# First mixer: the fill jobs around the heads multiplied in split form and in parts, four weight slots, and the second layer's modulation moved into the feed-forward stage

## The reference, cut to what matters

```python
# first block: one layer
proj = x @ w_in                       # da_q da_k da_v r_q r_k r_v r_g m_q and three gates
y_da  = diff_attention(da_q, da_k, da_v)          # 8 heads, two softmaxes a head
y_ret = silu(r_g) * retention(r_q, r_k, r_v)      # 4 heads
m_k, m_v = split(mem @ w_mem_kv)
y_mem = memory_attention(m_q, m_k, m_v)           # 4 heads
merged = sum_n(sigmoid(gate_n + b_gate_n) * (branch_n @ w_branch[n]))
x = layer_norm(alpha * x + merged @ w_o)
x = layer_norm(alpha * x + hier_moe(x))           # 16 experts, 2 per token
# second block: two layers; c is one row of 1024
for l in range(2):
    sh_m, sc_m, g_m, sh_f, sc_f, g_f = split(silu(c) @ ada_w[l] + ada_b[l])
    y = mixer_l(x * (1 + sc_m) + sh_m)            # even_mixer, then spatial gating
    x = layer_norm(alpha2 * x + (1 + g_m) * y)
    h = x * (1 + sc_f) + sh_f
    y = swiglu(h) if l == 0 else moe_swiglu(h)    # width 2816; then 8 experts of 3584
    x = layer_norm(alpha2 * x + (1 + g_f) * y)
```

## Time and profile before

| | us |
|---|---|
| median of 3 runs (2226.83 to 2230.08) | 2227.34 |
| the profiled execution | 2237.93 |
| its span, first to last instruction | 2236.1 |
| busy in the span: PE | 2138.5 (96%) |
| DVE | 1721.6 (77%) |
| ACT | 1383.4 (62%) |
| POOL | 29.9 (1%) |
| first mixer, to the first expert's chunks | about 535 |
| dense feed-forward stage | 932 to 1128 |

### The profile page before, as it was taken

The page is one execution under the profiler, slowest core; times in us unless marked ns, Lnnn a source line. Parts: engine busy times, 40 slices in busy tenths (PEclk is TensorE's granted clock), DMA queues, the critical chain, the costliest instruction groups (busy, mean ns, idle before and its releaser), DMA issues.

```text
span 2236.1 us, 26692 instructions
## 1 busy us (share of the span) xinstructions
PE 2138.5 (96%) x10668; PEld 1802.2 (81%) x10668; DVE 1721.6 (77%) x2065; ACT 1383.4 (62%) x1672; POOL 29.9 (1%) x30
## 2 busy tenths in 40 slices
PE   8999999989999988899988999999999999999997
PEld 7758889888888876778868888888888888888886
DVE  2566577777999876544456799999999999999988
ACT  3345344625778755443443678877877788878774
POOL 0000000000000000000000000000000000000000
PEclk9999999997999999899999799999999999999999
DMA  9656559547999973145440799999999999999994
GB/s 354 260 222 247 209 223 357 208 185 285 383 390 381 384 274 113 61 150 204 192 185 16 283 388 373 387 367 389 360 392 369 380 384 365 380 371 391 371 394 165
DMA packets 58071, 659.17 MB, mean 295 GB/s; under 512 B 6096, under 2 KB 12112, under 8 KB 18896
## 3 DMA queue, kind: packets, MB, share of 16 engines
q1 hardware_dynamic: 50832, 633.49, 72.8%
q0 software_dynamic: 3696, 13.63, 1.5%
q10 hardware_dynamic: 3408, 10.22, 1.2%
HBM read 645.79 MB, written 11.53 MB: 294 GB/s over the span
## 4 chain that ended last, share of the span: by engine, by line
PE 83%; DVE 9%; DMA 4%; ACT 3%; issue 2%; DVEq 0%; ACTq 0%; SPq 0%
PE psum L2193 55%; PE psum L1982 8%; PE psum L1940 7%; PE psum L1920 3%; DVE stage_lo L1700 2%; DMA ring<-moe_w_down_in 2%; PE psum L1972 2%; PE psum L2328 1%; PE psum L1899 1%; DVE ring L1363 1%; DMA ring<-moe_w_up_in 1%; DVE mixer_split L1467 1%; PE psum L2092 1%; PE psum L2203 1%; PE psum L2005 0%
## 5 line engine op out<-in xcount | busy, mean ns | idle before, releaser
L1700 DVE TENSOR_TENSOR stage_lo<-ring,stage_hi 128x1024 fp32r<-128x1024 f32 (+1 forms) x934 | 1099.4, 1217 | 107.7 <-ACT stage_hi L1245 94.0
L1245 ACT ACTIVATE stage_hi<-ring 128x1024 fp32r<-128x1024 f32 (+1 forms) x934 | 955.4, 1054 | 276.3 <-PE psum L2193 159.6
L2193 PE MATMUL psum<-stage_hi,x_hi 128*128 128x512 f32 (+1 forms) x1344 | 530.8, 395 | 3.6 <-DVE arena L1830 2.6
L2193 PE MATMUL psum<-stage_hi,x_lo 128*128 128x512 f32 (+1 forms) x1344 | 522.5, 389 | 0.0
L2193 PE MATMUL psum<-stage_lo,x_hi 128*128 128x512 f32 (+1 forms) x1344 | 521.0, 388 | 0.0
L2193 PEld LDWEIGHTS psum<-stage_hi,x_hi 128*128 128x128 f32 x1344 | 253.3, 188 | 53.8 <-issue 4.7
L2193 PEld LDWEIGHTS psum<-stage_hi,x_lo 128*128 128x128 f32 x1344 | 253.1, 188 | 53.5
L2193 PEld LDWEIGHTS psum<-stage_lo,x_hi 128*128 128x128 f32 x1344 | 253.6, 189 | 49.2
L2193 PE MATMUL psum<-stage_hi,h_hi 128*128 128x512 f32 x664 | 261.1, 393 | 2.7 <-DVE h_lo L1842 2.7
L2193 PE MATMUL psum<-stage_lo,h_hi 128*128 128x512 f32 x664 | 258.7, 390 | 0.0
L1940 PE MATMUL psum<-mixer_split 128*128 128x256 f32 x1184 | 194.3, 293 | 18.4 <-DVE mixer_split L1467 9.2
(11 more groups left out here) (264 smaller groups left out, 2091.1 us busy)
## 6 DMA issues: line engine op xcount, KB each, us to landing
ring<-moe_w_gate_in SPq DMA_DIRECT2D x56, 2048.0 KB, 9.8
ring<-moe_w_up_in SPq DMA_DIRECT2D x56, 2048.0 KB, 10.0
ring<-moe_w_down_in SPq DMA_DIRECT2D x56, 2048.0 KB, 9.9
ring<-w_in SPq DMA_DIRECT2D x48, 2048.0 KB, 9.9
ring<-ada_w_in SPq DMA_DIRECT2D x16, 2048.0 KB, 8.8
ring<-w_in_in SPq DMA_DIRECT2D x10, 2048.0 KB, 11.7
mixer_tiles<-w_in_in SPq DMA_DIRECT2D x9, 2048.0 KB, 9.6
mixer_tiles<-ada_w_in SPq DMA_DIRECT2D x8, 2048.0 KB, 8.8
```

Of the source, the lines that this page charges most:

```text
L1245: act.activation(chunk_view(stage_hi, f, side, p, c), chunk_source(f, side, p, c), ACT.Copy)\
L1700: dve.tensor_tensor(chunk_view(stage_lo, f, side, p, c), chunk_source(f, side, p, c), chunk_view(stage_hi, f, side, p, c).bitcast(F32), AL ...
L2193: ins = pe.matmul(dst, a, b, start=start, stop=stop)
```

## The change

Five things are done together.

1. All fill jobs of the attention heads, and m_q, become split jobs. `HEAD_FILL` gives each head its jobs, `HEAD_CHUNKS` their four chunks. New steps `("part", job, c)` let PE multiply one chunk at a time; the job's own gemm step does what is left. ACT's high parts are steps `("hi", job, c)` placed by hand among the parts of the head before, DVE's low parts of the first two chunks follow the norm, and those of the last two are made inside `da_score`, behind the maximum, while ACT takes the exponentials.
2. `da_turn` stands ahead of the head's last part instead of directly ahead of `da_out`.
3. The first mixer has four slots; the fifth one's place holds the four homes of high parts. The high part of x goes to mem's tile, so ACT loads mem later, at the first `("split", "x_late", 0)`. The stage of gate1 has no wait for the last `ret_out` any more.
4. Only the first layer's 12 ada panels stay in the first mixer: one between da_v's two pairs, one in each retention head, the rest from gate1 to the third memory head.
5. The second layer's modulation is made in the dense feed-forward stage. POOL loads 24 halves of panels, 1 MB each, into two buffers in the arena, each half when DVE has summed the one two before; DVE does one sum of 1024 behind each of 48 low parts (`sum_half`), and then bias and 1.

```diff
+HEAD_FILL = ((("r_q", 0), ("r_q", 1)), (("r_k", 0), ("r_k", 1)), (("r_v", 0),), (("r_v", 2),), (("r_g", 0), ("r_g", 1)),
+             (("r_g", 2), ("r_g", 3)), (("gate0", 0), ("gate0", 1)), (("gate0", 2), ("gate0", 3)))
+
+def chunks_in(job):
+
+    return 4 if job[0] in TURNED else 2
+
+HEAD_CHUNKS = [[(job, c) for job in jobs for c in range(chunks_in(job))] for jobs in HEAD_FILL]
...
+    def part(job, c):
+
+        if c < chunks_in(job) - 1:
+            return [("part", job, c)]
+        return gemms(job[0], *((job[1], job[1] + 1) if job[0] in TURNED else (job[1],)))
+
...
-    s += gemms("da_v", 0, 1, 2, 3) + [("lam", 0, 0)] + ada(0, 1)
-    fill = [q for name, n in (("r_q", 2), ("r_k", 2), ("r_v", 4), ("r_g", 4), ("gate0", 4)) for q in gemms(name, *range(n))]
+    s += gemms("da_v", 0, 1) + ada(0) + [(side, *HEAD_CHUNKS[0][c]) for side in ("hi", "lo") for c in range(2)]
+    s += gemms("da_v", 2, 3) + [("lam", 0, 0)] + [("hi", *HEAD_CHUNKS[0][c]) for c in (2, 3)]
     for h in range(DA_H):
-        s += [("da_score", h, 0), ("da_score", h, 1), fill.pop(0)]
+        now = HEAD_CHUNKS[h]
+        nxt = HEAD_CHUNKS[h + 1] if h + 1 < DA_H else []
+        s += [("da_score", h, 0), ("da_score", h, 1)] + [("hi", *q) for q in nxt[:1]] + part(*now[0])
+        s += part(*now[1]) + [("hi", *q) for q in nxt[1:2]]
         if h:
             s += [("da_norm", h - 1, 0)]
-        s += [fill.pop(0), ("da_turn", h, 0)] + ada(2 + h) + [("da_out", h, 0)]
+        s += [("lo", *q) for q in nxt[:2]] + part(*now[2]) + [("hi", *q) for q in nxt[2:3]]
+        s += [("da_turn", h, 0)] + part(*now[3]) + [("hi", *q) for q in nxt[3:4]] + [("da_out", h, 0)]
...
-        s += [fill.pop(0)] + ada(10 + h) + [("ret_mean", h, 0)]
+        s += [fill.pop(0)] + ada(1 + h) + [("ret_mean", h, 0)]
...
-        s += [("mem_out", h - 1, 0)] + ada(18 + h)
+        s += [("mem_out", h - 1, 0)] + (ada(9 + h) if h < 3 else [])
...
-        s += gemms("branch2", i) + splits("merged", i) + (ada(22 + i) if i < 2 else [])
+        s += gemms("branch2", i) + splits("merged", i)
...
-HI_HOMES = ([M_HI + n * 1024 for n in range(4)], [M_FREE + n * 1024 for n in range(4)],
+HI_HOMES = ([SLOT + n * 1024 for n in range(4)], [16384 + n * 1024 for n in range(4)],
...
-        plan_loads(n, SLOTS)
+        plan_loads(n, SLOTS if n else SLOTS - 1)
...
+        def half_loads():
+
+            pool.wait_ge(job_done, done[("ln_back", 2, 3)])
+            for j in range(24):
+                if j > 1:
+                    pool.wait_ge(ada_half_summed, j - 1)
+                nc.gpsimd.dma_start(ada_half[j % 2].rearrange("p a b -> p (a b)"),
+                                    w["ada_w_2"][1, j // 2][:, j % 2 * 2 * D:(j % 2 + 1) * 2 * D]).then_inc(ada_half_in[j % 2], 16)
...
+                        if i == 0:
+                            act.wait_ge(*last_use["x"])
+                            act.dma_start(memT.rearrange("p k t -> p (k t)"), w["mem"][0]).then_inc(mem_in, 16)
...
+        def sum_half(m):
+
+            j, c = m // 2, 48 + m
+            if m % 2 == 0:
+                dve.wait_ge(ada_half_in[j % 2], 16 * (j // 2 + 1))
+            wt = ada_half[j % 2][:, m % 2, :]
+            ins = dve.tensor_tensor_reduce(wt, wt, cond_row, 1.0, 0.0, ALU.mult, ALU.add, mod[:, c:c + 1])
+            if m % 2:
+                ins.then_inc(ada_half_summed, 1)
+            if m == 47:
+                dve.wait_ge(ada_half_summed, 24)
+                shift_modulation(1)
...
                     dve.tensor_reduce(dmax, logit, AX.X, ALU.max, negate=True).then_inc(da_logits, 1)
+                    job, c = HEAD_CHUNKS[a][2 + i]
+                    staged_low(("lo", *job), *staged_chunks(("lo", *job))[c])
                     dve.wait_ge(da_exped, u + 1)
...
+                    if not f["routed"] and 0 <= n - STAGES < 48:
+                        sum_half(n - STAGES)
```

More of the change, by code:

```diff
@@ L110, in shape_constants @@
     return out
-SPLIT = ("da_k", "da_v", "gate1", "m_k", "m_v", "branch1", "gate2", "branch2", "w_o")
-TURNED = ("da_v", "m_v", "ev_p", "od_v")
-SPLIT_OF = {"da_k": "x", "da_v": "x", "gate1": "x_late", "gate2": "x_late", "m_k": "mem", "m_v": "mem",
+SPLIT = ("da_k", "da_v", "m_q", "gate1", "m_k", "m_v", "branch1", "gate2", "branch2", "w_o")
+TURNED = ("da_v", "r_v", "m_v", "ev_p", "od_v")
+HEAD_FILL = ((("r_q", 0), ("r_q", 1)), (("r_k", 0), ("r_k", 1)), (("r_v", 0),), (("r_v", 2),), (("r_g", 0), ("r_g", 1)),
[3 more added lines that the diff above has]
+HEAD_CHUNKS = [[(job, c) for job in jobs for c in range(chunks_in(job))] for jobs in HEAD_FILL]
+SPLIT_OF = {"da_k": "x", "da_v": "x", "r_q": "x", "r_k": "x", "r_v": "x", "r_g": "x", "gate0": "x", "m_q": "x", "gate1": "x_late", "gate2": "x_late", "m_k": "mem", "m_v": "mem",
             "branch1": "yret", "branch2": "ymem", "w_o": "merged", "ev_q": "h1", "ev_p": "h1", "ev_o": "mix1",
@@ L125, in with_stages @@
     jobs = [n for n, q in enumerate(steps) if q[0] == "gemm" and not (q[1] in TURNED and q[2] % 2)]
+    made = [q[1] if q[0] == "hi" else q[1:] for q in steps if q[0] in ("hi", "stage")]
     at = {}
     for before, n in zip(jobs, jobs[1:]):
-        if steps[n][1] not in SPLIT:
+        if steps[n][1] not in SPLIT or steps[n][1:] in made:
             continue
@@ L170, in mixer1_steps @@
         s += [("ret_out", h, 0)] + (splits("x_late", 0, 1, 2, 3) if h == RET_H - 1 else [])
-        s += [fill.pop(0)] + ada(10 + h) + [("ret_mean", h, 0)]
+        s += [fill.pop(0)] + ada(1 + h) + [("ret_mean", h, 0)]
         s += ([("ret_score", h + 1, 0)] if h + 1 < RET_H else []) + [fill.pop(0), ("ret_var", h, 0)]
-    s += gemms("gate1", 0, 1) + splits("mem", 0, 1, 2, 3) + gemms("gate1", 2, 3) + ada(14)
-    s += gemms("m_k", 0, 1) + ada(15) + gemms("m_k", 2, 3) + ada(16)
-    s += gemms("m_v", 0, 1) + ada(17) + gemms("m_v", 2, 3) + splits("yret", 0, 1, 2, 3) + ada(18)
+    s += gemms("gate1", 0, 1) + splits("mem", 0, 1, 2, 3) + gemms("gate1", 2, 3) + ada(5)
+    s += gemms("m_k", 0, 1) + ada(6) + gemms("m_k", 2, 3) + ada(7)
+    s += gemms("m_v", 0, 1) + ada(8) + gemms("m_v", 2, 3) + splits("yret", 0, 1, 2, 3) + ada(9)
     s += [("mem_score", 0, 0)] + gemms("branch1", 0)
@@ L402, in build @@
     cond_row = scratch(M_ADA, D)
+    ada_half = [region(at, 2, D) for at in (R_K, R_V)]
     router = (small[:, 160:320].rearrange("p (k e) -> p k e", e=G1 + N1),
@@ L471, in build @@
     ada_summed = sem("ada_summed")
+    ada_half_in, ada_half_summed = [sem(f"ada_half_in{n}") for n in range(2)], sem("ada_half_summed")
     w_hi_set, w_lo_set, w_used = sem("w_hi_set"), sem("w_lo_set"), sem("w_used")
@@ L547, in build @@
         for s in plan:
-            if s[0] in ("ada", "stage", "hi", "lo", "split", "lam", "sg_norm"):
+            if s[0] in ("ada", "stage", "hi", "lo", "part", "split", "lam", "sg_norm"):
                 continue
@@ L913, in _ @@
             for k, one in enumerate(loads[n]):
-                if n == 0 and k == SLOTS:
+                if n == 0 and k == SLOTS - 1:
                     small_loads()
@@ L1005, in walk @@
                     for n, c in staged_chunks(q) if kind == "stage" else staged_chunks(q)[i:i + 1]:
-                        if s == ("stage", "gate1", 0):
-                            act.wait_ge(job_done, done[("ret_out", RET_H - 1, 0)])
                         if hi_free[n]:
@@ L1011, in walk @@
                     continue
-                if kind in ("lo", "sg_norm"):
+                if kind in ("lo", "part", "sg_norm"):
                     continue
@@ L1327, in _ @@
             act.wait_ge(job_done, plan_end[n])
[L1328 removed]
+            act.wait_ge(ada_summed, 12)
             if feeds[n]["routed"]:
@@ L1901, in turn4, with split_product @@
             ins.then_inc(job_done, 1)
-        def split_product(s):
+        opened = {}
+        def split_product(s, parts):
             _, a, i = s
@@ L1909, in split_product @@
                 nxt = ("gemm", a, i + 1)
-                banks = [open_bank(s), open_bank(nxt)]
-                for n, c in staged_chunks(s):
+                if 0 in parts:
+                    opened[s] = [open_bank(s), open_bank(nxt)]
+                banks = opened[s]
+                for n, c in [staged_chunks(s)[m] for m in parts]:
                     pe.wait_ge(w_lo_set, n + 1)
@@ L1926, in split_product @@
                 return
-            if s == ("gemm", "ev_o", 0):
+            if s == ("gemm", "ev_o", 0) and 0 in parts:
                 for m in range(2):
@@ L1931, in split_product @@
                     evacuated(("gqa_out", n, 0))
-            b = open_bank(s)
-            for m, (n, c) in enumerate(staged_chunks(s)):
+            if 0 in parts:
+                opened[s] = open_bank(s)
+            b = opened[s]
+            for m, (n, c) in [(m, staged_chunks(s)[m]) for m in parts]:
                 pe.wait_ge(w_lo_set, n + 1)
@@ L1945, in _ @@
         pe.wait_ge(ones_set, 2)
+        begun = {}
         def walk(plan):
@@ L1948, in walk @@
```

(7 more changed lines are left out.)

21 lines of the change are left out of this document (12 added, 9 removed).

## The result

The changed kernel takes 2211.64 us (median of 4 runs, 2208.3 to 2213.78), the kernel before 2228.71 in the runs beside it: ratio 0.9919, 95% interval 0.9905 to 0.9932, a gain of 17 to 18 us. A second comparison (`after_again`) gave 0.9907 (0.9892 to 0.9922), some 21 us. Faster, then, but by about half of the 37 us forecast. The profiled execution has a span of 2211.9 us against 2236.1.

What follows compares the result with a forecast made beforehand. PE, nearly always busy, was taken to bound the kernel by its work and few holes. Terms -9.1 - 9.9 - 8.0 - 4.7 - 12.5 + 1 + 6 = -37.2 gave 2200.7 profiled, 2190 timed; forecast 2182 to 2198, range 2176 to 2213.

Steps and rivals of the forecast that it cites:

- heads: Attention heads: split fill jobs and moved ada panels save 9.1 us in head 0, 9.9 in 1-3, 8.0 in 4-7.
- retention heads: Retention: four m_q jobs become split jobs and DVE's work still fits under PE's, -4.7 us.
- tail behind the memory heads: End of the memory branch: without three ada panels, PE's holes and the clock drop go, -12.5 us.
- four slots: First mixer's panel queue: m_k's second panel and gate2's are asked for late, +1 us, bounds 0 and 4.
- feed-forward stage: Dense feed-forward: sums are free, but DVE waits for contended half loads, +6 us, bounds 0 and +36.
- The bound of 4: First mixer: the most, in us, that going to one slot fewer was expected to cost.
- By hand through one pair: Feed-forward pair walked: two waits of about 3 us, 3.5 free, about 2.4 left, in 2.6 pairs: +6.
- the upper bound: Feed-forward with all half loads contended: 12 x 14.2 = 170 against PE's 134 us, +36.
- Half loads or ACT bind harder: Rival: feed-forward waits of 20 us and more, or ACT stretching the heads; gain 8 to 28, 2199 to 2219; chance 0.26.
- All hidden: Rival: PE also sets heads 4 to 7 at 14.6 each, loads are free; -51, 2176 us; chance 0.17.
- The slower one: Rival: each feed-forward half load takes 15.8 us, +97, 2281 us; decides above 11.3 us average; chance 0.05.
- The split paid: Opposite of a rival where parts wait for low parts, heads keep 17 us, about 2208; no chance of its own.

Runs made afterwards that it cites:

- after_again: The changed kernel itself, unaltered, run once more beside the kernel before: 2212.81 us, 0.9907 of the kernel before.
- turn_late: The changed kernel with the heads' turn behind the last part, straight ahead of its products: 2222.99 us, 0.9953 of the kernel before.
- before_slots4: The kernel before with only its first mixer's panels going round four slots in place of five: 2236.67 us, 1.0017 of the kernel before.
- five_slots: The changed kernel with four half buffers, panels taking the first free slot, and a fifth slot from the last m_q job: 2189.81 us, 0.9809 of the kernel before.
- four_buffers: The changed kernel with four half-load buffers in place of two, so four loads are under way: 2193.54 us, 0.9821 of the kernel before.

## Why the forecast of 37 us became 17

Stretch by stretch on the two profiled executions, forecast against measured:

| step | forecast | measured |
|---|---|---|
| heads (149.66 us before) | -27.0 | -29.7 |
| retention heads | -4.7 | -3.2 |
| tail behind the memory heads | -12.5 | -12.8 |
| four slots: up to memory head 0, and in the memory heads | +1 | +2.7 +3.5 |
| feed-forward stage | +6 | +16.6 |
| stretches whose work did not change | 0 | -1.6 |
| sum | -37.2 | -24.5 (spans: -24.2) |

**Heads: right.** Head 0 15.0 us (forecast 14.7), heads 1 to 3 14.3 each (14.75), heads 4 to 7 62.06 together (63.8). I had put the handover of ACT and DVE a hair over PE in heads 1 to 3; it came out a hair under, 14.08 against 14.3. (By the forecast's own terms a head with silu adds up to 16.5, not 16.1, and eight heads at 14.6 save 32.9, not the 33.3 of the rival; neither matters.) In heads 4 to 6 ACT does set the pace, by two further table loads in each. The changed kernel's chain there:

```profile
169.41 1.28 ACT L1127
...
172.02 0.60 ACT mixer_tiles L1028
...
172.66 1.13 PE psum L2071 x4
```

The table load, then the copy of the turn, then PE, which had waited. The turn ahead of the last part is worth 9 us of the 29.7 (`turn_late`).

**Tail: right**, with its clock: 26.14 us at 1.00, the higher level, 2.4 GHz. The low parts no longer stand behind an ada panel's sums, 1.2 us of the 8.9 of hole are left, and the fall to 0.50 does not come.

**Retention** came 1.5 us short. The trace has it in the first retention head (0.8 us ahead of its first products, 0.7 in its jobs), where the chain still runs through the norm and the low parts behind the last attention head; no run took it apart.

**Four slots: the mechanism was right, the size was not**, 6.2 us in place of 1. I had named the two tightest panels, m_k's and gate2's, and set 7 us of lead against a landing of 7.8. The panels landed in 8.4, 11.5 and 9.1 us, and there was a third, branch1's first. The bound of 4 that I kept was too low. `before_slots4` (+6.1 us from the first head's scores to the norm's turns) and `five_slots` (4.3 to 6.3 less than the changed kernel and `four_buffers`) show the size from both sides.

**Feed-forward stage: the step that failed.** "By hand through one pair: two waits of about 3 us, of which 3.5 are free: about 2.4 us left, in 2.6 pairs". The runs show three waits, 10.3 us, of which some 3.5 are free: 6.8 and 6.6 in two pairs, and 4.8 before the first h_lo, where I had counted nothing, because the third load (requested at 911.73, landed at 921.0) held the sums, the low parts behind them, and then the first h. A later pair gave 1.5 back. The landing itself I had not underestimated: I took 10.8 us for a contended load, and the ten loads that DVE waited for took 6.8 to 9.7, nine of them 8.5 or more. The waits of 3 us do not follow from the forecast's own terms: 10.8 less the 5.7 allowed is 5.1, two of those less 3.5 free are 6.7 a pair, and 2.6 pairs of that are 17, near the 16.6 measured, though there it was three shorter waits a pair and not two. So the walk through one pair is what failed. DVE works in its own rhythm: a buffer is asked for behind its second sum and wanted two sums and three low parts later, 5.4 us (972.29 plus 5.4 is where DVE stopped, 4.27 us ahead of the landing). Each cycle of two buffers then takes a landing and 3.8 us more, 13.4 us for four chunks, against 10.9 on PE; three cycles are the pair of 40.35. That sum stood in my prediction, with 10.8 + 3.44, but as the upper bound instead of the model. Even the 7.8 us of a 2 MB panel in it would have given 11.2 a cycle, over PE's 10.9.

What decides is the number of buffers: a third allows two chunks more, some 5 us, and the cost is gone while the landing is longer.

The Trainium skill, SBUF — State Buffer, section "SBUF: two separate sides", warns of VectorE operations in a two-port mode that delay GpSimd's descriptors. No such delay shows here: the first packet came after 1.2 us with VectorE busy, and after 3.7 to 4.1 only behind a panel. The Trainium skill, DMA: Bandwidth & Descriptors, section "Queues, rings and completion order", has each DMA engine take turns between queues packet by packet. From that I had drawn a landing of 8.3 us. The 8.5 to 9.7 of nine of the loads that were waited for lie nearer to that than to my 10.8, but even turns are not what the trace shows: 84 packets of the panel and none of the half load in the first 3.8 us. Whether the half load's descriptors were late or no turns were taken, no run here tells. The time that I drew from it, 0 to 2, was wrong all the same, since a landing of 8.3 is 2.9 over the 5.4 allowed.

**The base.** The gain of the two spans is 24.2 us, that of the medians 17.1 (15.2 to 21.2). I carried an offset of 10.6 us from the profiled execution to the median over to the changed kernel; its profiled execution (2213.78 us) lay only 2.1 above its median. Stretches with the same work differ between kernels here: from the first norm's turns to the second mixer's group of 144 matmuls ahead of its norm 389.7 us before, 393.9 in the changed kernel, 390.1 and 391.6 with four and three buffers. But the changed kernel's second profile (`after_again`) has 390.4 there, so this is the spread from one execution to the next and not the kernel. So some 7 us of the miss are not in any term; what makes these stretches vary was not tested, and a term of the table that is smaller than some 4 us carries little.

**The rivals.** "Half loads or ACT bind harder" held, on its half-load side alone: 2211.6 in 2199 to 2219. "All hidden" failed twice: heads 4 to 7 took 62.06 us and not 58.4, and the loads were not free. The slower one did not come: the half loads never averaged near 11.3 us. The split paid: heads of 14.3 to 16.2 us, not 17. With both losses taken away (`five_slots`) the kernel takes 2189.8 us. That this is the forecast of 2190 is luck: the forecast held 7 us for the two losses, and without them would have been 2183.

## What to carry to other kernels

For a transfer in a ring of buffers, write down the cycle first: landing under the traffic of that stage, plus the work between landing and next request, against the time the bounding engine gives to as many chunks. If it doesn't fit, the engine's idle time covers a part of the difference and the rest is lost, cycle after cycle; another buffer costs nothing where memory is free in that stage. Look also at what else is asked for just before it: here every late load stood 1.4 us behind a panel. A slot taken from a queue of panels is dear where the queue is in order and some of its entries are freed late by another engine, and it can be given back as soon as what took its place is dead. And a sum made from one profiled execution is better set against a second one before its distance to the median is carried over.

## What the runs showed of the hardware that was not expected

- The same 1 MB loads landed in 7.6 us by the median (5.1 to 9.6) from GpSimd's queue and in 6.6 (5.0 to 9.1) from SyncE's, beside the same panels. GpSimd's issue took 0.53 us, SyncE's 0.33. The Trainium skill, DMA: Bandwidth & Descriptors, section "Latency and other measured facts", gives about 0.4 us between the two ways for the first byte. With no panel flowing the first packet came 1.2 us after the request from GpSimd's queue (938.74) and 0.97 from SyncE's, and the loads landed in 5.15 and 5.0: 0.3 us and less. The rest arises beside the panels.
- A 1 MB load asked for from GpSimd's queue 1.4 us behind a 2 MB panel of SyncE's had no packet for 3.7 to 4.1 us, while the panel's ran at full stream; with a 1 MB panel ahead of it 2.55 us. What serves the panel first no run shows.
- More loads under way landed later (9.4 us with three buffers, 9.6 with four) and did no harm: what counts is that they were asked for earlier.
